# Two gated projections as seven block products, over two halves of the tokens

## The reference

```python
h  = rms_norm(x, g_pre) * (1 + scale) + shift           # (2048, 1024)
uv, z = split(h @ w_in_o)                               # u, v, z: (2048, 2048) each
u, v = gelu(uv);  v = layer_norm(v, g_ln, b_ln)
mixed = einsum('gij,bnjgc->bnigc', w_s, vc) + b_s       # 8 groups, chunks of 128 tokens
y = (u * mixed * silu(z)) @ w_out_o
x = x + gate * rms_norm(y, g_post)
```

## Time and profile before

| | |
|---|---|
| median of 3 runs | 3066.03 us (3062.02 to 3066.72) |
| span of the profiled execution | 3062.0 us |
| TensorE busy | 2971.0 us (97%), 16548 matmul records |
| VectorE, ScalarE, GpSimd busy | 1403.8, 1162.5, 700.4 us |
| value stage's last matmul to the first output matmul | 1946.9 to 2703.2 us |

### The profile page before, as it was taken

How to read it: one execution, slowest core, us unless ns; L and a number is a source line. 1 busy time by engine, 2 the same in 40 slices (tenths; PEclk the granted TensorE clock), 3 DMA queues, 4 the chain that set the end, 5 groups by cost and what they waited for, 6 DMA issues and landing times.

```text
span 3062.0 us, 46947 instructions
## 1 busy us (share of the span) xinstructions
PE 2971.0 (97%) x16548; PEld 2477.5 (81%) x16548; DVE 1403.8 (46%) x2513; ACT 1162.5 (38%) x2093; POOL 700.4 (23%) x738
## 2 busy tenths in 40 slices
PE   4999999999999999999999999999999999999998
PEld 4768888788788888887878888888888888888887
DVE  6577777855777777773254111223222222222011
ACT  4652254554555555553154111233332332322111
POOL 0212111366333333322320001012111211123221
PEclk8999999999999999999999999999999999999999
DMA  7243355586212111115542221212211221145231
GB/s 267 64 126 102 108 165 163 187 270 184 73 55 60 55 55 55 55 55 193 167 147 97 97 75 48 73 62 72 72 62 62 69 75 62 55 151 165 83 110 55
DMA packets 259931, 317.64 MB, mean 104 GB/s; under 512 B 17188, under 2 KB 187300, under 8 KB 257223
## 3 DMA queue, kind: packets, MB, share of 16 engines
q1 hardware_dynamic: 259816, 316.10, 31.7%
HBM read 213.67 MB, written 102.37 MB: 103 GB/s over the span
## 4 chain that ended last, share of the span: by engine, by line
PE 85%; issue 4%; DVE 4%; POOL 3%; ACT 2%; DMA 1%; SPq 0%; DVEq 0%; POOLq 0%; ACTq 0%
PE PS L344 12%; PE PS L346 12%; PE PS L345 12%; PE PS L2367 4%; PE PS L2368 4%; PE PS L2369 4%; PE PS L1795 4%; PE PS L2518 4%; PE PS L2520 4%; PE PS L2519 4%; PE PS L1773 4%; PE PS L1796 2%; PE PS L2695 2%; PE PS L1763 2%; PE PS L1764 2%
## 5 line engine op out<-in xcount | busy, mean ns | idle before, releaser
L344 PE MATMUL PS<-hTh,whi 128*128 128x512 f32 x1664 | 658.2, 396 | 1.5 <-DVE hTl L298 1.1
L346 PE MATMUL PS<-hTh,wlo 128*128 128x512 f32 x1664 | 649.1, 390 | 0.0
L345 PE MATMUL PS<-hTl,whi 128*128 128x512 f32 x1664 | 648.8, 390 | 0.0
L344 PEld LDWEIGHTS PS<-hTh,whi 128*128 128x128 f32 x1664 | 313.2, 188 | 76.9 <-DVE hTl L298 6.3
L346 PEld LDWEIGHTS PS<-hTh,wlo 128*128 128x128 f32 x1664 | 312.9, 188 | 66.1
L345 PEld LDWEIGHTS PS<-hTl,whi 128*128 128x128 f32 x1664 | 313.4, 188 | 62.6 <-issue 0.2
L334 POOL TENSOR_TENSOR whi<-wraw,zero 128x1024 fp32r<-128x1024 f32 x50 | 95.7, 1913 | 1163.9 <-PE PS L346 934.0
L1876 ACT ACTIVATE pb__167<-PS,nm,rq 128x512 f32<-128x512 f32 x256 | 197.4, 779 | 103.6 <-DVE nm L1939 103.6
L2367 PE MATMUL PS<-ow_h,of_h 128*128 128x512 f32 x576 | 224.4, 390 | 1.9 <-DVE oy L2318 1.9
L2369 PE MATMUL PS<-ow_h,of_l 128*128 128x512 f32 x576 | 224.1, 389 | 0.0
L2368 PE MATMUL PS<-ow_l,of_h 128*128 128x512 f32 x576 | 224.1, 389 | 0.0
(11 more groups left out here) (273 smaller groups left out, 5605.4 us busy)
## 6 DMA issues: line engine op xcount, KB each, us to landing
projT<-pev SPq DMA_DIRECT2D x80, 256.0 KB, 2.7
xt<-x SPq DMA_DIRECT2D x8, 2048.0 KB, 8.7
mw<-wmod SPq DMA_DIRECT2D x64, 256.0 KB, 2.8
oxt<-x SPq DMA_DIRECT2D x32, 512.0 KB, 4.7
sg_v<-vev SPq DMA_DIRECT2D x64, 256.0 KB, 2.4
wraw<-wuz SPq DMA_DIRECT2D x32, 512.0 KB, 5.6
vm<-sg_v SPq DMA_DIRECT2D x16, 1024.0 KB, 5.5
sgT<-mT SPq DMA_DIRECT2D x16, 1024.0 KB, 4.4
```

The lines of the kernel that those rows point to most:

```text
L344: pe.matmul(PS[:, bank, :], w[1][:, s, k, :], hTh[:, k, b], start=(k == 0), stop=False)
L345: pe.matmul(PS[:, bank, :], w[1][:, s, k, :], hTl[:, k, b], start=False, stop=False)
L346: mm = pe.matmul(PS[:, bank, :], w[2][:, s, k, :], hTh[:, k, b], start=False, stop=(k == KD - 1))
```

## The change

It makes the two outputs of a column tile by a block scheme. The weights of a column tile are seen as 2 x 2 blocks A (z or u, first or second half of the 1024 contraction rows), h as 2 x 2 blocks B (half of the contraction rows, one or the other token block of 512 in a half of 1024 tokens). The four result blocks are had from seven products of sums of blocks (12 matmuls each: four contraction blocks, three matmuls) in place of eight (the form of Strassen's scheme by Winograd). The stage becomes 32 units: for each half of the tokens (`h`), for each pair of column tiles (`i`), for each tile of it (`u`).

- The sums of h (blocks of 128 x 512) are made once by GpSimd during the value slabs (`part_sums`), stored in HBM (`hc`) by DMAs that GpSimd issues, and read back in 44 parts through four buffers `hst`: 16 in the last slab, 28 around the change of halves. ScalarE writes the high part over h in SBUF, VectorE the low part (`part_load`, `part_hi`, `part_lo`). The first 16 overwrite later tokens; so slabs 1 to 3 take tokens 1024 to 2047 first (`v_tile`).
- The weights are loaded by two DMAs a unit (`pair_load`, 512 KB each, into `wpr`), GpSimd makes four sums of 128 x 512, ScalarE seven high parts (`pair_hi`), GpSimd seven low parts (`pair_lo`), one unit ahead of the products.
- Products 4 to 6 accumulate onto what lies in PSUM; between them VectorE adds banks to SBUF (`zu2`, `zu3`, `zT`, `uT`). Mixing is eight matmuls a unit, behind product 3. Gelu and Silu run mostly from SBUF.
- The column sums move into the first unit, behind product 2. `sw` is loaded later. The output stage's first two weight rows and `sgT` pieces are prepared in the last unit, the third not before the last product of the gated stage.

The diff, cut to its core:

```diff
+        def v_tile(n, p):
+            return p if isinstance(n, int) and n == 0 else (p + NT // 2) % NT
+        def part_slots(p):
+            return range(3 * (p - 9), min(16, 3 * (p - 8))) if p >= 9 else ()
...
+            for p in range(NT):
+                store(NV - 1, p)
+                if p == 0:
+                    pair_load(sp, (0, 0, 0), 0, False)
+                for m in part_slots(p):
+                    part_load(sp, m)
...
+        def part_sums(pool):
+            pool.wait_ge(s_hl, 64)
+            for half in range(2):
+                for kk in range(4):
...
+                    sum_(1, t1, blk_of(hTh, 0, 1), blk_of(hTh, 0, 0), ALU.subtract)
...
+                    sum_(10, t4, t4, blk_of(hTl, 4, 0), ALU.add, 9)
+                    pool.wait_ge(s_tq, E_tq + first + 10)
+                    pool.dma_start(hc[half, 1:5, kk].rearrange("i p c -> p i c"), tq[:, :, :]).then_inc(s_tqs, 16)
...
+        def part_load(sp, m):
...
+            if m >= 4:
+                sp.wait_ge(s_hcl, E_hcl + m - 3)
+            sp.dma_start(hst[:, m % 4, :], hc[half, idx, kk]).then_inc(s_hst[m % 4], 16)
...
+        def pair_load(sp, j, ahead, wait=True):
+            h, i, u = j
+            if wait:
+                sp.wait_ge(s_wcl, E_wcl + cnt(j, 7, 7 * ahead))
...
+            for s in range(2):
+                sp.dma_start(wpr[:, s, :, :].rearrange("p a c -> p (a c)"), a["wuz"][ds(c + s, 1), :, :].rearrange("a p f -> p (a f)")
+                             ).then_inc(s_wpr[s], 16)
+
+        def pair_sums(pool, j, ahead):
+            for s in range(2):
+                pool.wait_ge(s_wpr[s], E_wpr + cnt(j, 16, 16 * ahead + 16))
+            pool.tensor_tensor(wsx[:, 0, :], A21, A22, ALU.add).then_inc(s_ws, 1)
+            pool.wait_ge(s_ws, E_ws + cnt(j, 4, 4 * ahead + 1))
+            pool.tensor_tensor(wsx[:, 1, :], wsx[:, 0, :], A11, ALU.subtract).then_inc(s_ws, 1)
+            pool.tensor_tensor(A21, A11, A21, ALU.subtract).then_inc(s_ws, 1)
...
+        def pair_hi(act, j, ahead, k):
...
+                act.wait_ge(s_pp, E_pp + cnt(j, 7, k + 1))
...
+            act.activation(w_part(k, 0), W_SRC[k], ACT.Copy).then_inc(s_wch, 1)
+
+        def pair_lo(pool, j, ahead, k):
+            pool.wait_ge(s_wch, E_wch + cnt(j, 7, 7 * ahead + k + 1))
+            pool.tensor_tensor(w_part(k, 1), W_SRC[k], w_part(k, 0).bitcast(F32), ALU.subtract).then_inc(s_wcl, 1)
...
 def uz_sp: unit(j)
+                parts(ending, *range(16, 20))
+                parts(opening, *range(32, 36))
+                if not last:
+                    pair_load(sp, j, 1)
+                if not first:
+                    store(before(j))
+                parts(ending, *range(20, 28))
+                parts(opening, *range(36, 44))
+                if not last:
+                    load_v(j, 1)
+                parts(ending, *range(28, 32))
...
 def uz_act: unit(j)
+                def hi(k):
+                    if not last:
+                        pair_hi(act, j, 1, k)
+                    if ending and k < 4:
+                        for m in range(16 + 4 * k, 20 + 4 * k):
+                            part_hi(act, m)
+                    if opening and k < 3:
+                        for m in range(32 + 4 * k, 36 + 4 * k):
+                            part_hi(act, m)
...
+                act.activation(zu2[:, :], PS[:, 2 + u, :], ACT.Copy).then_inc(s_zp, 1)
...
+                for t in range(NT // 2):
...
+                hi(0)
+                hi(1)
+                hi(2)
+                act.wait_ge(s_zc22, E_zc22 + cnt(j, 1, 1))
+                act.activation(zT[1][:, :], zT[1][:, :], ACT.Silu).then_inc(s_zs, 1)
+                hi(3)
...
 def uz_dve: unit(j)
+                dve.scalar_tensor_tensor(sbias[:, :], srow[:, g], sgb[:, c], sbs[:, g], ALU.mult, ALU.add).then_inc(s_zsb, 1)
+                parts(opening, 32)
+                dve.wait_ge(s_zp, E_zp + cnt(j, 1, 1))
+                dve.wait_ge(s_pp, E_pp + cnt(j, 7, 2))
+                dve.tensor_tensor(zu2[:, :], PS[:, 4, :], zu2[:, :], ALU.add).then_inc(s_zu, 1)
+                parts(ending, 16)
+                parts(opening, 36)
+                dve.wait_ge(s_zu, E_zu + cnt(j, 2, 1))
+                dve.wait_ge(s_pp, E_pp + cnt(j, 7, 3))
+                dve.tensor_tensor(zu3[:, :], PS[:, 5, :], zu2[:, :], ALU.add).then_inc(s_zu, 1)
+                parts(opening, 40)
...
 def uz_pe
+            def product(j, k):
+                h, i, u = j
+                bank = (2 + u, 4, 5, 6, 5, 6, 2 + u)[k]
+                pe.wait_ge(s_wcl, E_wcl + cnt(j, 7, k + 1))
+                if h:
+                    pe.wait_ge(s_hcl, E_hcl + 16 + 4 * (k + 1))
...
+                elif k == 4:
+                    pe.wait_ge(s_zu, E_zu + cnt(j, 2, 2))
...
+                for kk in range(4):
+                    hh, hl = h_tile(hTh, k, kk), h_tile(hTl, k, kk)
+                    pe.matmul(o, wc[:, k, 0, kk, :], hh, start=(kk == 0 and not onto), stop=False, skip_group_check=onto)
+                    pe.matmul(o, wc[:, k, 0, kk, :], hl, start=False, stop=False, skip_group_check=onto)
+                    mm = pe.matmul(o, wc[:, k, 1, kk, :], hh, start=False, stop=(kk == 3), skip_group_check=onto)
...
+                    for k in range(7):
+                        product(j, k)
+                        if k == 2 and is_unit(j, 0, 0, 0):
+                            column_sums()
+                        if k == 3:
+                            mixed(j)
```

More of the change, by code:

```diff
@@ L2307, in out_dve @@
             o = O_W[l]
[L2308 removed]
+            for k in range(2 * l, OK[l]):
                 out_dve_w(dve, l, k)
@@ new lines, in emit @@
+        wsx = at("wsx", X0 + 66 * K, [P, 2, 512])
+        tq = at("tq", X0 + 58 * K, [P, 4, 512])
+        zu2 = at("zu2", H0 + 10 * K, [P, 512])
+        zu3 = at("zu3", H0 + 74 * K, [P, 512])
+        uT = [at("uT%d" % b, H0 + (18 + 64 * b) * K, [P, 512]) for b in range(2)]
+        zT = [at("zT%d" % b, H0 + (26 + 64 * b) * K, [P, 512]) for b in range(2)]
+        s_tq, E_tq = s_msx, 5 * NT
+        s_zw = sem("s_zw")
+        s_tqs, E_tqs = sem("s_tqs"), 0
+        s_hst, E_hst = s_ml, 8 * NT
@@ new lines, in emit, with cnt, unit_loop @@
+        s_zu, E_zu = s_mx, NU
+        s_zc22, E_zc22 = s_mq, NU
+        s_zc21, E_zc21 = s_mlb, NU
+        s_zc12, E_zc12 = s_bx, NT
+        s_zg, E_zg = s_bt, NT
+        s_zs, E_zs = s_bkT, NT
+        s_zmu, E_zmu = s_bc, NT - 1
+        s_zst, E_zst = s_bv, NT
+        def cnt(j, per, add=0):
+            h, i, u = j
+            return i * (2 * per) + ((CT * h + u) * per + add)
+        def unit_loop(eng, pair):
+            for h in range(2):
+                pair(h, 0)
+                with eng.Fori(1, CT // 2 - 1) as i:
+                    pair(h, i)
+                pair(h, CT // 2 - 1)
@@ new lines, in pair_lo, with load_v, store, before @@
+        def pair_lo(pool, j, ahead, k):
+            pool.wait_ge(s_wch, E_wch + cnt(j, 7, 7 * ahead + k + 1))
+            pool.tensor_tensor(w_part(k, 1), W_SRC[k], w_part(k, 0).bitcast(F32), ALU.subtract).then_inc(s_wcl, 1)
+        def uz_sp(sp):
+            def load_v(j, ahead):
+                h, i, u = j
+                if ahead:
+                    sp.wait_ge(s_zmx, E_zmx + cnt(j, 2, 2))
+                    sp.wait_ge(s_zc, E_zc + 48)
+                if ahead and is_unit(j, 0, CT // 2 - 1, 1):
+                    h, c = 1, 0
+                else:
+                    c = i * 2 + (u + ahead)
+                sp.dma_start(vm[:, :, :], sg_v[h * S // 2:(h + 1) * S // 2, ds(c * P, P)].rearrange("(t p) c -> p t c", p=P)
+                             ).then_inc(s_zv, 16)
+            def store(j):
+                h, i, u = j
+                sp.wait_ge(s_zmu, E_zmu + cnt(j, 4, 4))
+                sp.wait_ge(s_zc, E_zc + 48)
+                sp.dma_start(sgT[ds(i * 2 + u, 1), :, h * S // 2:(h + 1) * S // 2].rearrange("a p f -> p (a f)"),
+                             mT[:, :, :].rearrange("p b f -> p (b f)")).then_inc(s_zst, 16)
+            def before(j):
+                h, i, u = j
+                if is_unit(j, 1, 0, 0):
+                    return (0, CT // 2 - 1, 1)
+                return (h, i, 0) if u else (h, i - 1, 1)
+            def unit(j):
+                first, last = is_unit(j, 0, 0, 0), is_unit(j, 1, CT // 2 - 1, 1)
+                ending, opening = is_unit(j, 0, CT // 2 - 1, 1), is_unit(j, 1, 0, 0)
+                def parts(on, *ms):
+                    if on:
+                        for m in ms:
+                            part_load(sp, m)
+                parts(ending, *range(16, 20))
[9 more added lines that the diff above has]
+                parts(ending, *range(28, 32))
+            def pair(h, i):
+                for u in range(2):
+                    unit((h, i, u))
```

498 lines of the change are left out of this document (313 added, 185 removed).

## The result

The changed kernel takes 3025.89 us (median of 4 runs, 3017.93 to 3033.21); the kernel before, on the same chip, 3064.16 (3062.02 to 3066.72). The ratio is 0.9877 [0.9861, 0.9893]: 38 us or 1.2% faster. The forecast was 3016 us, with a range of 2986 to 3052. The profiled execution of after has a span of 3031.4 us, one of the two slower of its runs; that of before 3062.0.

A forecast was written before the change was run, and what follows sets the result against it. TensorE was taken to bound the kernel, so time falls with its matmuls. 4.1 + 666.6 + 5 + 22 = 697.7 us against 756.2, with +10 and -1.5, gave -50 us: 3016 us, range 2986 to 3052.

The forecast's parts named there:

- Part 1: Gated stage on TensorE: 168 matmuls per column tile in place of 192, 20.83 us a unit, 666.6 us for 32 units.
- Rival D: Products of twelve matmuls with two or three waits each don't hide the sequencer: 0.1 us per product, 3038 us; chance 0.06.
- Parts 2 and 3: Engine loads per unit and the single-buffered weights' loop through GpSimd: period 21.1 us against TensorE's 20.83, 5 us lost.
- Part 4: Entry of the gated stage, with the column sums behind product 2 and a wait for `srow`: 4.1 us.
- Part 5: Turn between the halves: reloading 28 parts of h makes `zu3` late, 22 us lost, from 10 to 30 (GpSimd already behind).
- Part 6: Value slabs: splits of the value weights meet GpSimd's `part_sums`, 10 us for two slabs, 0 if GpSimd stands in a transfer.
- Part 7: Exit to the output stage: the wait of 1.54 us for the second output weight goes, third row just there, -1.5 us.
- The sum: Stage 697.7 us against 756.2; with value slabs and exit -50 us, a profiled span of 3012, 3016 against the median.
- A: TensorE sets all: the weights' loop fits, the turn costs 10 us and the splits 0; 2989 us, chance 0.16.
- B: The weights' loop sets the pace at 22.3 us a unit, with a turn of 28 us; 3051 us, chance 0.19.
- C: Slower: all eleven GpSimd operations per unit meet a VectorE one, period 24.1 us, 3100 us; tipping point 23.0; chance 0.07.

The follow-up runs named there:

- e5: Changed kernel with one more GpSimd operation per unit, the low part of the first weight block being written twice: 3086.36 us.
- e6: Changed kernel with VectorE's four SBUF-by-SBUF multiplications per unit (mT by uT and by zT) cut to 8 of 512 columns: 3004.70 us.
- e2: Changed kernel with the weights' second block row (A21, A22) loaded as soon as low part 4 is written: 3007.08 us.
- e8: As e7, with operands of the second half's products 4 to 6 split earlier around the turn and the stage's last store two places later: 2992.94 us.
- e7: Changed kernel with h's high parts ahead of the weights' on ScalarE around the turn, and A21 and A22 loaded two low parts earlier: 2998.65 us.
- e11: As e7, with VectorE's 28 subtractions for the low parts of the second half's operands cut from 512 to 8 columns: 2992.40 us.
- e12: As e11, with ScalarE's 28 copies for the high parts of the second half's operands cut to 8 columns too: 2990.24 us.

## Why the prediction was right, and where it wasn't

The forecast lay 10 us under the result, and the mechanism was the one named. That it came so near is in part luck: the terms of the gated stage were 18 us too small and the value slabs' term 10 too large.

- **Part 1, the matmuls.** Right to a hundredth: 20.84 in place of 20.83 us a unit, wherever nothing waits. Rival D is out, twelve matmuls a product cost nothing extra.
- **Parts 2 and 3, the loop.** 21.29 in the period shown and 21.53 as the mean, against 21.1. The GpSimd part was 15.4 us (forecast 14.3 + 1.6 = 15.9; its 1.21 us between independent operations was read from a pair whose second is a cast, and between two with two inputs it is 1.25 here), the load with its hand-overs 5.9 to 6.2 (forecast 5.2), since the store and the `vm` load travel beside it. The lock was a little dearer (0.45 in place of 0.35 us) and hit three operations, not five: the last of the four products waited for GpSimd's last operation and kept no other, and the bias (0.34 us at 2120.39) ran while GpSimd waited for its load. The first half lost 10.4 us and the second none, against 5 forecast for both. I had counted the lead from the turn for 4 to 6 us; the stall was longer, so it lasted all fourteen units. e5, e6 and e2 lengthen, shorten and unload this loop, and TensorE's pace follows each time.
- The Trainium skill (SBUF — State Buffer, "SBUF: two separate sides") says that the pair of ports is an exclusive lock between a VectorE operation with two SBUF inputs and a GpSimd operation that reads SBUF. This case's runs agree: such VectorE operations go by turns with GpSimd's, those with one input from PSUM keep their 0.68 us.
- **Part 4, the entry.** Forecast 4.1, measured 5.1: the wait for `srow` was 2.5 us in place of 1.7.
- **Part 5, the turn.** The largest miss: 31.7 us against 22, just over the end of 30. `zu3` was the right sum to wait for and the opening unit the right unit. But the ending unit, which I took to be held only by its last high part, had a stall of 10.8 of its own for the same sum: its first four parts came behind weight copy 0, which waited for its load until 2299 in that unit. By the prediction's own count, the `wpr` of the opening unit landed 50.6 us after TensorE began the ending unit (2333.6 against 2283.0) and not 41, and from there to the end of both units it was 22.7 against 22.5: the whole miss lies ahead of that landing. The condition of the upper end, GpSimd already behind, was met: where GpSimd comes to the turn ahead (e2), it costs 8.3 us less. And I left out the clock, 4.2 us.
- **Part 6, the value slabs.** Wrong: +10 forecast, 0.1 measured. The splits did lengthen,

```profile
1686.23 8.49 DVE L2489 TENSOR_TENSOR vsl<-vsr,vsh 128x512 fp32r<-128x512 f32 x8
```

  8.49 us in place of 5.48, and 6.42 at the next slab. But GpSimd's own timeline has it in its transfer's wait just then:

```profile
1684.61 0.78 POOL L2669 DMA_DIRECT2D hc<-tq  x1 [0.31 <-POOL tq L2654]
1689.51 1.27 POOL L2654 TENSOR_TENSOR tq<-hTh 128x512 f32<-128x512 f32 x1 [4.12 <-DMA hc<-tq]
```

  so only the later half of the eight met it, and TensorE had the 3 us of slack to cover that (before, the eighth split ended at 1684.74 and was needed about 1688.5). I had named this case and given it the lower end. `part_sums` issued its last transfer at 1829.0, inside the forecast 1810 to 1835; there are sixteen transfers and not twelve, in twelve waits.
- **Part 7, the exit.** Wrong in sign: -1.5 forecast, +2.6 measured over the output stage. The store of the last `mT` stands in SP's queue ahead of the loads for row 2, and GpSimd is late. e8's later store ends e7's wait of 2.1, and in e6 it is 0.2 in place of 2.9. The wait of 0.88 for the last Gelu I had not counted.
- **The sum.** Extras over 666.6 us: forecast 31.1 in the stage; measured 716.0 - 666.6 = 49.4, which are 5.1 + 10.4 + 31.7 and about 2 of small waits. That is 18 us more. The value slabs gave 10 back and the exit took 4: 12 us over the forecast. With the 7.0 us by which this execution was late beforehand, these are the 19.4 between its span of 3031.4 and the forecast 3012; the medians are 10 apart.
- **The rivals.** A (all hidden, 2989) is what the corrected versions come near, e8 with 2992.94. B had a turn of 28, which was nearly right, with a loop of 22.3, which was not. C would have needed a period of 23.0: e5, at 23.36 to 23.49 us, crossed that point and was indeed slower than the kernel before, by 0.7%. So its tipping point is borne out by one run beyond it. Its condition is not: three operations of eleven met VectorE, in e5 four of twelve, and not all.

## What to carry to other kernels

When TensorE's work is cut, write down the period of every loop that closes through a single buffer (load, use, last read, next load) and compare it with TensorE's new period: a difference of 0.7 us in 21 was worth 10 us here, and starting the half of the load whose readers are done two operations earlier won 19. Look for VectorE operations with two SBUF inputs beside a GpSimd engine that has become part of that loop. And in a one-off phase such as a refill between two halves, walk through each engine's queue unit by unit; what counts is what stands ahead of the one sum that the next matmul needs, not the load of the engines.

## What the runs showed of the hardware

- Under contention VectorE and GpSimd took turns by whole operations: GpSimd's 1.29 became 1.74 to 1.76 us, VectorE's 0.69 became 1.67 to 1.78. A 128 x 8 subtraction of VectorE's took 0.17 us in the median and up to 1.2 to 1.25 at the turn (e11, e12).
- After a stall of 10.8 us and one of 15.5 us the matmuls started 0.43 us apart for about twelve and nine of them before they were back at 0.227; after a stall of 11.9 us in e8 the 16 mixing matmuls took 3.75 us in place of 1.95. Short waits went either way: after 2.48 us (`srow`, after) the matmuls kept the upper clock, after 2.49 (e5, at 2135.93, granted clock 0.50) six started 0.43 us apart. The row of e8:

```profile
2309.16 3.75 PE L3013 MATMUL PS<-sw,vm 128*128 128x128 f32 x16 [11.85 <-ACT vm L2871]
```

- A load of 256 KB landed in 3.2 us (median), one of 32 KB in 1.8: an eighth of the bytes saved less than half of the time.
- A transfer issued by GpSimd itself took 0.77 to 1.0 us of its queue for 1 MB, with a wait of 3.7 to 4.4 us behind it.
